# The first weight sum of the gate and up groups: a copying and an adding DMA transfer in place of a GpSimd addition

## The reference, cut to what matters

```python
def swiglu_ffn(h, w_gate, w_up, w_down):
    return (jax.nn.silu(h @ w_gate) * (h @ w_up)) @ w_down
```

## Time and profile before

| | |
|---|---|
| three executions | 1060.91, 1060.92 and 1060.92 us, median 1060.92 |
| span of the profiled execution, first to last instruction | 1059.4 us |
| granted TensorE clock, mean | 1.000 |
| TensorE busy (matmuls) | 1052.7 us, 99% |
| VectorE busy | 800.7 us, 76% |
| ScalarE busy | 496.4 us, 47% |
| GpSimd busy | 223.4 us, 21% |
| transfers, mean share of the 16 DMA engines | 33.3% from SyncE's queue, 0.4% from GpSimd's |

### The profile page before, as it was taken

How to read it: one execution, slowest core, us unless ns; L and a number is a source line. 1 busy time by engine, 2 the same in 40 slices (tenths; PEclk the granted TensorE clock), 3 DMA queues, 4 the chain that set the end, 5 groups by cost and what they waited for, 6 DMA issues and landing times.

```text
span 1059.4 us, 17927 instructions
## 1 busy us (share of the span) xinstructions
PE 1052.7 (99%) x6290; PEld 922.5 (87%) x6290; DVE 800.7 (76%) x1200; ACT 496.4 (47%) x762; POOL 223.4 (21%) x211
## 2 busy tenths in 40 slices
PE   9999999999999999999999999999999999999997
PEld 8888888999999998888878766789999999988887
DVE  5755659999999999544465677599999999975453
ACT  6312236644444546222247777466545445552222
POOL 6000001223322320222110366003233232102010
PEclk9999999999999999999999999999999999999999
DMA  7333242233333232432436602113323323342321
GB/s 202 116 90 113 81 118 80 80 119 95 103 119 103 95 110 81 138 94 82 127 110 148 149 23 60 40 41 120 113 85 119 119 80 118 111 114 82 112 65 80
DMA packets 144075, 106.85 MB, mean 101 GB/s; under 512 B 4488, under 2 KB 140096, under 8 KB 144032
## 3 DMA queue, kind: packets, MB, share of 16 engines
q1 hardware_dynamic: 143392, 104.80, 33.3%
q0 software_dynamic: 608, 1.47, 0.4%
q10 hardware_dynamic: 32, 0.01, 0.0%
HBM read 99.98 MB, written 2.10 MB: 96 GB/s over the span
## 4 chain that ended last, share of the span: by engine, by line
PE 99%; DVE 0%; ACT 0%; issue 0%; DVEq 0%; POOL 0%; ACTq 0%; POOLq 0%
PE ps L454 26%; PE ps L456 26%; PE ps L455 25%; PE ps L1836 4%; PE ps L1855 4%; PE ps L1971 3%; PE ps L1839 2%; PE ps L1858 2%; PE ps L2032 2%; PE ps L2048 2%; PE ps L2134 1%; PE ps L1706 1%; PE ps L2138 0%; PE ps L1695 0%; PE ps L2013 0%; PE ps L2015 0%
## 5 line engine op out<-in xcount | busy, mean ns | idle before, releaser
L456 PE MATMUL ps<-x_op,op_w_lo 128*128 128x256 f32 x896 | 253.5, 283 | 0.0
L454 PE MATMUL ps<-x_op,op_w_hi 128*128 128x256 f32 x896 | 253.4, 283 | 0.0
L455 PE MATMUL ps<-x_op,op_w_hi 128*128 128x256 f32 x896 | 253.3, 283 | 0.0
L454 PE MATMUL ps<-hid_hi,wgt 128*128 128x512 f32 x476 | 186.6, 392 | 0.0
L456 PE MATMUL ps<-hid_hi,wgt 128*128 128x512 f32 x476 | 185.3, 389 | 0.0
L455 PE MATMUL ps<-hid_lo,wgt 128*128 128x512 f32 x476 | 185.3, 389 | 0.0
L437 DVE TENSOR_TENSOR wgt<-raw,wgt 128x1024 fp32r<-128x1024 f32 (+3 forms) x110 | 119.1, 1098 | 74.7 <-ACT wgt L420 73.8
L454 PEld LDWEIGHTS ps<-x_op,op_w_hi 128*128 128x128 f32 x896 | 171.3, 191 | 1.2 <-issue 1.1
L456 PEld LDWEIGHTS ps<-x_op,op_w_lo 128*128 128x128 f32 x896 | 171.4, 191 | 0.0
L455 PEld LDWEIGHTS ps<-x_op,op_w_hi 128*128 128x128 f32 x896 | 171.3, 191 | 0.1
L739 POOL TENSOR_TENSOR w_sum<-pair_raw 128x512 f32<-128x512 f32 x42 | 55.6, 1325 | 488.3 <-DMA pair_raw<-in_ffn_w_gate 304.1
(11 more groups left out here) (246 smaller groups left out, 1648.0 us busy)
## 6 DMA issues: line engine op xcount, KB each, us to landing
pair_raw<-in_ffn_w_gate SPq DMA_DIRECT2D x22, 1024.0 KB, 5.3
pair_raw<-in_ffn_w_up SPq DMA_DIRECT2D x22, 1024.0 KB, 5.3
raw<-in_conv_w_in SPq DMA_DIRECT2D x24, 512.0 KB, 3.7
raw<-in_ffn_w_down SPq DMA_DIRECT2D x28, 384.0 KB, 3.3
raw<-in_ffn_w_down SPq DMA_DIRECT2D x28, 320.0 KB, 3.0
raw<-in_conv_w_out SPq DMA_DIRECT2D x8, 512.0 KB, 3.7
raw<-in_mla_w_o SPq DMA_DIRECT2D x8, 512.0 KB, 3.9
raw<-in_ffn_w_down SPq DMA_DIRECT2D x5, 512.0 KB, 4.8
```

The costliest lines, as they stand in the source:

```text
L454: nc.tensor.matmul(acc, wh, xh, start=first, stop=False)
L455: nc.tensor.matmul(acc, wh, xl, start=False, stop=False)
L456: return nc.tensor.matmul(acc, wl, xh, start=False, stop=last)
```

## The change

In the 40 half-groups of the loop, s1 gets a buffer of its own, `s1_sum`, with a place for each of the two matrices. GpSimd issues a transfer of A21 from HBM into it, waits for its landing, and issues a second transfer that adds A22 to it (`accum_op=ALU.add`): in layer 0 from HBM, right after the first; in layer 1 from the raw weights in SBUF, and so after the load of this half-group has landed. Then GpSimd computes s2 as before. The splits of part 1 become two instructions on ScalarE and two on VectorE, since s1 no longer lies beside s2 and s3. In the first pair the additions stay, and write into the new buffer.

```diff
+        s1_sum, _, _ = place("s1_sum", [P, 2, S], F32, HID + DC * S * 4)
...
             if part == 1:
-                return slice(1, 4), w_sum[:, 0:3, :].rearrange("p n (c m) -> p n c m", m=P)
+                return slice(2, 4), w_sum[:, 1:3, :].rearrange("p n (c m) -> p n c m", m=P)
...
+            if part == 1:
+                nc.scalar.activation(four(op_w_hi[:, 1:2, :]), first_sum(par), ACT.Copy)
             nc.scalar.activation(four(op_w_hi[:, slots, :]), src, ACT.Copy).then_inc(op_hi, PART_SIZE[part])
...
+            if part == 1:
+                nc.vector.tensor_tensor(four(op_w_lo[:, 1:2, :]), first_sum(par), four(op_w_hi[:, 1:2, :]).bitcast(F32),
+                                        ALU.subtract)
             nc.vector.tensor_tensor(four(op_w_lo[:, slots, :]), src, four(op_w_hi[:, slots, :]).bitcast(F32),
                                     ALU.subtract).then_inc(op_lo, PART_SIZE[part])
...
-                wait(pool, pair_in[par], i * 16 + 16 * (PAIRS_F * l + 1))
-                if not isinstance(free, int) or free >= 0:
-                    wait(pool, op_lo, free + 4)
-                    wait(pool, sum_done, done)
-                nc.gpsimd.tensor_tensor(wide(w_sum, 0), b["A21"], b["A22"], ALU.add).then_inc(sum_done, 1)
...
+                m = (gates, ups)[par][l]
+                col = ds(i * (2 * P), P)
+                turn = i * 16 + 16 * (PAIRS_F - 1) * l
+                wait(pool, op_lo, free + (4 - OPS))
+                wait_apart(pool, sum_done, done)
+                pool.dma_start(wide(s1_sum, par), m[:, 0:DC:2, col]).then_inc(s1_first[par], 16)
+                wait_apart(pool, s1_first[par], turn)
+                if l == 0:
+                    pool.dma_start(wide(s1_sum, par), m[:, 1:DC:2, col], accum_op=ALU.add).then_inc(s1_both[par], 16)
+                wait_apart(pool, pair_in[par], i * 16 + 16 * (PAIRS_F * l + 1))
+                if l == 1:
+                    pool.dma_start(wide(s1_sum, par), b["A22"], accum_op=ALU.add).then_inc(s1_both[par], 16)
+                wait(pool, op_lo, free + 4)
+                wait(pool, sum_ve, done)
+                wait(pool, s1_both[par], turn)
+                nc.gpsimd.tensor_tensor(wide(w_sum, 1), wide(s1_sum, par), b["A11"], ALU.subtract).then_inc(sum_done, 2)
...
-                nc.vector.tensor_tensor(wide(w_sum, 0), b["A21"], b["A22"], ALU.add).then_inc(sum_done, 1)
+                nc.vector.tensor_tensor(wide(s1_sum, 1), b["A21"], b["A22"], ALU.add).then_inc(sum_done, 1)
                 third_sum(l, 0, 1)
                 ve.wait_ge(sum_done, done + 1)
-                nc.vector.tensor_tensor(wide(w_sum, 1), wide(w_sum, 0), b["A11"], ALU.subtract).then_inc(sum_done, 1)
+                nc.vector.tensor_tensor(wide(w_sum, 1), wide(s1_sum, 1), b["A11"], ALU.subtract).then_inc(sum_done, 1)
```

More of the change, by code:

```diff
@@ L270, in trunk_kernel @@
         pair_in = [sem("pair_in_gate"), sem("pair_in_up")]
+        s1_first, s1_both = [sem("s1_first_gate"), sem("s1_first_up")], [sem("s1_both_gate"), sem("s1_both_up")]
         sum_done, sum_ve, op_hi, op_lo, op_used = sem("sum_done"), sem("sum_ve"), sem("op_hi"), sem("op_lo"), sem("op_used")
@@ L596, in trunk_kernel, with first_sum @@
         READY = [1, 4, 4, 4, 7, 5, 7]
+        def first_sum(par):
+            return s1_sum[:, par:par + 1, :].rearrange("p n (c m) -> p n c m", m=P)
         def four(part):
@@ L734, in weight_sums @@
                 free = op_no(l, i, par, 0) - OPS
-                wait(pool, pair_in[par], i * 16 + 16 * (PAIRS_F * l + 1))
-                if not isinstance(free, int) or free >= 0:
-                    wait(pool, op_lo, free + 4)
-                    wait(pool, sum_done, done)
-                nc.gpsimd.tensor_tensor(wide(w_sum, 0), b["A21"], b["A22"], ALU.add).then_inc(sum_done, 1)
-                if not isinstance(free, int) or free >= 0:
-                    wait(pool, op_lo, free + 4)
-                    wait(pool, sum_ve, done)
@@ L743, in weight_sums @@
-                wait(pool, sum_done, done + 1)
-                nc.gpsimd.tensor_tensor(wide(w_sum, 1), wide(w_sum, 0), b["A11"], ALU.subtract).then_inc(sum_done, 1)
+                if isinstance(free, int):
+                    wait(pool, pair_in[par], i * 16 + 16 * (PAIRS_F * l + 1))
+                    if free >= 0:
+                        wait(pool, op_lo, free + 4)
+                        wait(pool, sum_done, done)
+                    nc.gpsimd.tensor_tensor(wide(s1_sum, par), b["A21"], b["A22"], ALU.add).then_inc(sum_done, 1)
+                    if free >= 0:
+                        wait(pool, sum_ve, done)
+                    wait(pool, sum_done, done + 1)
+                    nc.gpsimd.tensor_tensor(wide(w_sum, 1), wide(s1_sum, par), b["A11"],
+                                            ALU.subtract).then_inc(sum_done, 1)
+                    return
```

## The result

The changed kernel takes 1109.77 us (1108.5 to 1110.92), before 1060.92: ratio 1.046, 95% interval 1.0445 to 1.0475. The forecast was 1097, with a range to 1140.

The account below looks back on a forecast made before the run. TensorE, busy 99%, bounds the kernel at 9.99 us per half-group. An 11.0 us GpSimd chain over 19 steps, plus late first beats, less 4.3 cover, gives 18.8 + 17.7 = 36.5 us: 1097 us, range 1060.4 to 1140.

Parts of the forecast that it names:

- The mechanism and the beat: GpSimd's in-order queue: copy, landing, adding transfer, landing, s2 take 11.0 us per half-group, 1.0 over TensorE's 9.99.
- The adding transfer's engine time: On the DMA engines: the adding transfer reads both operands, so its packets count twice, 1.8 us against a copy's 0.9.
- The terms of the chain: On GpSimd, per half-group: copy 4.1 us, adding transfer 5.0, s2 1.6 and handoffs 0.3.
- rival A: GpSimd's chain fits the beat if both transfers land in 8.1 us together: no change, 1060.9 us; chance 0.37.
- "512" descriptors: GpSimd's software issue: 512 descriptors per transfer instead of 48 to 128 add an estimated 0.6 us to each.
- The rival by a page: By the skill's fit, each GpSimd transfer takes 2.6 us and the chain about 7.1, so the no-change case would hold.
- Handoffs: In GpSimd's chain: three handoffs by semaphore at 0.1 us each, 0.3 in all.
- The first beat: The first copy waits for VectorE's second sum, so the first s2 is 3.9 us late in layer 0, 2.8 in layer 1.
- The cover of 4.3 us: s2 can be late by 2.8 + 0.2 + 1.3 = 4.3 us, once in a layer, before TensorE stops.
- Splits and VectorE: Part 1's extra splits cost nothing: at most 0.62 us on ScalarE, 0.14 on VectorE, covered; VectorE's 128x512 low split shrinks toward 677 ns.
- The wait for the load in layer 1: In GpSimd's chain, layer 1's adding transfer also waits for the half-group's load; no size of its own.
- X: Time of GpSimd's chain per half-group, forecast 11.0 us; s2 comes every max(X, 9.99); 12.2 was the range's upper end.

Follow-up runs that it names:

- the first experiment: Against the changed kernel, GpSimd adds s1 itself in every half-group, with no transfer; the own buffer and part 1's split instructions stay: 1061.16 us, ratio 1.000.

## Why the prediction was right, and where it was short

**The mechanism and the beat: right.** The chain on GpSimd, in order and without overlap, was forecast at 11.0 us and is 11.1 to 11.2. That the chain and not the traffic or the splits is the cause is shown from both sides: one landing less gives back 42 us, the copy ahead with the load's wait out of the way gives back all, one landing more costs 195. The adding transfer's engine time, which no row of before had, was put at 1.8 us, twice a copy's 0.9. The queue's share was 11.9% of 16 x 1109.2 us with 40 adding transfers and 7.0% of 16 x 1075.0 with copies in their place: 908 us more, 1.4 per transfer and engine. On a copy's 0.9 (the 7.0%, less the kernel before's 0.4%, over 80 copies) that makes 2.3.

**The terms of the chain: two mis-sized, and they cancel by luck.** The prediction summed times to landing, 4.1 and 5.0, and handoffs of 0.3. In the half-group at 262.51 the landings took 3.3 and 4.6, s2 1.5, and the handoffs 0.7 (s2 to the copy), 0.7 (copy landed to the next issue) and 0.2: 11.0 in all. The landings were put 1.2 us too high, the handoffs 1.3 too low. With the landings as measured and the handoffs as forecast the sum is 3.3 + 4.6 + 1.5 + 0.3 = 9.7, under the beat. That is rival A, whose condition, both landings within 8.1 us together, came true (7.9), and only the handoffs kept it from the result. Of the copy's 0.8 too much, 0.6 had been added for "512" descriptors; its 512 runs went as 80 packets.

**The rival by a page.** The copy landed 3.3 us after its issue and the adding transfer 4.6. The Trainium skill, DMA: Bandwidth & Descriptors, Anatomy of one DMA, has a fit of a transfer's time; worked out for this size it gives an estimate of 2.6 us. This trace does not agree, for a transfer of 512-byte runs.

**Handoffs: mis-sized.** "Three handoffs by semaphore at 0.1" are 0.66 to 0.85 us between s2's end and the copy's issue, 0.7 between the copy's landing and the next issue, and 0.2 ahead of s2. The 1.3 us more, over 38 beats, would be 49 us, the size of the whole loss.

**The first beat: mis-sized.** The first copy in layer 0 went out at 195.43 and not at 194.4, 0.8 us after VectorE's sum ended at 194.62, and the first s2 ended at 205.01 + 1.29 = 206.30, 4.8 late instead of 3.9.

**The cover of 4.3 us: the step that failed in layer 0.** It was read in a settled half-group. What counts is the cover at the first one, where s2 ended at 201.46 and product 1 started at 208.53, 12 starts of 0.12 before product 2 at 209.97. In the changed kernel product 1 starts 3.6 us after s2's end (209.88 - 206.30), so the cover there was 7.1 - 3.6 = 3.5. In the changed kernel's trace this first product 1 comes 1.35 us later than before (209.88 against 208.53). The last one of the layer comes 23.3 later (421.53 against 398.27), so the 19 beats between add 21.9; they are 11.14 us in the mean, some longer than the 11.10 shown. A wait for the first low part of the next stage adds 1.6. That makes 24.8 us, as much as layer 0 costs alone (24.8), where 18.8 were forecast.

**The first beat of layer 1: not foreseen.** The copy there took 5.90 us (747.70 - 741.80) and the adding transfer 7.85, so this one chain is 15.0 us long instead of 11. The timeline of GpSimd in the changed kernel:

```profile
741.80 0.81 POOL L762 DMA_DIRECT2D s_sum<-in_ffn_w_gate  x1 [25.83 <-DVE op_w_lo L625]
747.70 1.34 POOL L768 DMA_DIRECT2D s_sum<-pair_raw  x1 [5.10 <-DMA s_sum<-in_ffn_w_gate]
755.55 1.26 POOL L772 TENSOR_TENSOR w_sum<-s_sum,pair_raw 128x512 f32<-128x512 f32 x1 [6.52 <-DMA s_sum<-pair_raw]
```

and two stretches there, us busy of PE, PEld, DVE, ACT and POOL, then granted clock, DMA share, GB/s:

```profile
752.00:764.00 12.00, 6.90 (x43) 6.50 (x42) 6.49 (x11) 6.17 (x8) 3.36 (x3) 0.76 0.39 80
764.00:780.00 16.00, 16.00 (x118) 15.29 (x117) 12.38 (x19) 5.32 (x9) 4.84 (x4) 0.96 0.71 165
```

TensorE waited 5.1 us at once, and its granted clock fell from 1.00 to a mean of 0.76 and then 0.96 in the two stretches. From 760 to 764 us it was 0.50, the 1.2 GHz level. The 12 matmuls of product 1 and the first four of product 2 took 4.44 us (760.38 to 764.82) instead of 2.37, so the clock cost 2.1 us. The load of the next half-group was issued at 748.11, in the midst of it. The queues from 747.7 to 752.7 us, and then from 752.7 to 755.2:

```profile
q1 hardware_dynamic: 881, 0.90, 63.3%
...
q0 software_dynamic: 528, 0.26, 84.0%
```

No packet of the adding transfer moved in the first five microseconds, while 881 of the load did. So it was slow because it stood behind a load, as in the run without the copy (7.69) and with the third transfer (5.98). The first use of this path in the layer is not the cause: in the run without the copy it is as slow in every half-group of layer 0 from the third on. In the changed kernel's trace the layer costs 25.0 us: 5.4 at its first product 1, 18.1 over 19 beats of 10.94 (the clock's 2.1 among them), 1.6 at the end. Alone it cost 22.9 us, where 17.7 were forecast.

**Splits and VectorE: right.** The splits cost nothing. VectorE's 128x512 low split fell from 1049 to 683 ns and its 1024 form from 1387 to 1219, once nothing of GpSimd's ran beside them (with GpSimd's additions kept, in the first experiment, the 1024 form stays at 1388 from 200 to 390 us):

```profile
L625 DVE TENSOR_TENSOR op_w_lo<-pair_raw,op_w_hi 128x1024 fp32r<-128x1024 f32 x18 | 21.9, 1219 | 0.0
...
L625 DVE TENSOR_TENSOR op_w_lo<-w_sum,op_w_hi 128x512 fp32r<-128x512 f32 x18 | 12.3, 683 | 0.0
```

The Trainium skill, SBUF — State Buffer, Who interferes with whom, says that a VectorE instruction with two inputs in SBUF contends with a GpSimd instruction that reads SBUF; the trace agrees. It saved time on an engine that TensorE didn't wait for in the kernel before.

**The wait for the load in layer 1: called part of the chain, and it isn't.** Read alone it was harmless (the run with HBM in both layers did not gain). It is the second limit, at 10.3 to 10.5 us, that shows only when the first is gone. The prediction's chain had no such loop through the load and VectorE's order.

**A slip in the range.** At X = 12.2 the prediction's own sum gives 1145 us and not 1141; nothing hangs on it.

## What to carry to other kernels

An operation of 1.3 us on an engine that nobody waits for was replaced by two dependent transfers, whose price is their landing and the handoffs around it: about 4 us for a 256 KB copy and 4.8 for an adding one, from issue to GpSimd's next instruction and one after the other. Before such a step, sum the whole chain from one round to the next on the issuing engine and compare it with the beat of the bound engine; 11.1 against 9.99 is most of the result (38 x 1.1 = 42 of the 49 us), and issuing one round ahead brings it back to 1061.5 us. Sum the handoffs as carefully as the landings. Keep the adding transfer's issue clear of a large load's. Then look for the next loop, which runs through the buffer that the transfer waits for, and take the cover from the first round and not from a settled one.

## What the runs showed of the hardware that was not expected

- A transfer from GpSimd that adds has 528 packets for 512 runs of 512 bytes, a copy of the same shape 80. From SyncE's queue the copy has 528 as well (21120 more on that queue for 40 copies). On GpSimd the adding one's issue takes 1.29 us against 0.75 to 0.80, and it ends 1.35 us later than a copy.
- The same adding transfer of 256 KB took from 4.3 to 7.85 us. With a load of 1 MB issued close to it, its packets began 3.0 to 5.2 us after the issue; with none in its way, 1.9 to 2.0.
- Where a transfer from GpSimd followed s2 on the same engine, it began 0.66 to 0.85 us after it, and where it followed the landing of a transfer, 0.7. In both places waits and an increment of a semaphore stand in between. Which of these takes the time was not tried. Ahead of s2, with plain waits, it is 0.2.
- Waits of TensorE of 0.85 us in every half-group left the granted clock at 1.00; one of 5.1 us, and waits of 3 to 5 us in every half-group, did not.
